# Two expert layers: router logits taken by tokens, one low part moved behind the choice, the first gather cut in two

## The reference

```python
def _hier_moe(x, w_grp, b_grp, w_exp, b_exp, w_gate, w_up, w_down):
    grp_logits = (xf @ w_grp + b_grp).astype(F32)           # 4 groups
    g_idx = jnp.argmax(grp_logits, axis=-1)
    exp_logits = (xf @ w_exp + b_exp).reshape(n, N_GROUPS, EXPERTS_PER_GROUP)   # 8 in each
    in_grp = take(exp_logits, g_idx)
    top_l, top_e = lax.top_k(in_grp, TOP_K_IN_GROUP)        # 2 experts of the token's group
    gate = p_grp * softmax(top_l)
    ...
    hdn = silu(xb @ w_gate[e]) * (xb @ w_up[e])             # 1024 -> 512, tokens of expert e
    y   = hdn @ w_down[e]                                   # 512 -> 1024, added back with its weight
```

## Time and profile before

| what | value |
|---|---|
| median of the runs | 2326.71 us (2326.80, 2326.71, 2320.91) |
| span of the profiled execution | 2323.1 us (the page gives no other time of that execution) |
| PE busy, PE weight loads | 2166.1 us (93%), 1528.0 us (66%) |
| DVE, ACT, POOL busy | 1142.2 us (49%), 784.0 us (34%), 61.5 us (3%) |
| loaded from memory | 619.5 MB, 267 GB/s over the span |
| mean granted clock of PE | 0.975 |
| experts of layer 0 and 1 | about 184 to 640 us, and 831 to 1291 us |

### The profile page before, as it was taken

One profiled execution on the slowest core, in us unless ns is written; L12 is line 12 of the kernel. 1 busy time (PEld: TensorE's weight loads), 2 busy tenths in 40 slices (PEclk: granted clock), 3 DMA queues, 4 the chain that ended last, 5 costly groups with the idle time before them and its releaser, 6 DMA issues.

```text
span 2323.1 us, 30109 instructions
## 1 busy us (share of the span) xinstructions
PE 2166.1 (93%) x12126; PEld 1528.0 (66%) x12126; DVE 1142.2 (49%) x1786; ACT 784.0 (34%) x1299; POOL 61.5 (3%) x62
## 2 busy tenths in 40 slices
PE   8999998899887989997988999999999999989998
PEld 7884443443367944433433688898888788888887
DVE  5582222121156831211111666678666766787666
ACT  3441110111034321101111355454555455554553
POOL 0010000000010100000000000001000000001000
PEclk9999999899998799999999999999999999999999
DMA  9449999999972289999999864634555464534561
GB/s 289 145 175 379 421 421 421 417 421 420 413 246 73 76 363 420 420 421 415 420 420 421 295 209 168 199 128 127 181 200 200 154 208 166 193 96 159 167 208 46
DMA packets 231542, 622.66 MB, mean 268 GB/s; under 512 B 15456, under 2 KB 166944, under 8 KB 182112
## 3 DMA queue, kind: packets, MB, share of 16 engines
q1 hardware_dynamic: 226096, 605.32, 68.7%
q0 software_dynamic: 3040, 10.78, 1.5%
q10 hardware_dynamic: 2256, 4.50, 0.5%
HBM read 619.51 MB, written 1.05 MB: 267 GB/s over the span
## 4 chain that ended last, share of the span: by engine, by line
PE 41%; DMA 6%; DVE 4%; ACT 2%; issue 1%; POOL 0%; SPq 0%; DVEq 0%; ACTq 0%
PE bank L1517 14%; PE bank L1505 10%; PE bank L1518 7%; PE bank L228 6%; PE bank L1345 3%; DMA arena<-in_moe_w_up 1%; DMA ring<-in_moe_w_up 1%; DMA ring<-in_ffn_gate 1%; DMA w_parts<-in_moe_w_up 1%; DMA x_tok<-in_moe_w_up 1%; DVE w_low L439 1%; PE bank L1673 1%; ACT w_high L432 1%; DVE x_tok L687 0%; DVE x_tok L676 0%
## 5 line engine op out<-in xcount | busy, mean ns | idle before, releaser
L439 DVE TENSOR_TENSOR w_low<-ring,w_high 128x1024 fp32r<-128x1024 f32 x364 | 441.1, 1225 | 271.7 <-ACT w_high L432 271.7
L1517 PE MATMUL bank<-xT_parts,w_high 128*128 128x512 f32 x1408 | 496.2, 395 | 6.0 <-DVE xT_parts L504 6.0
L432 ACT ACTIVATE w_high<-ring 128x1024 fp32r<-128x1024 f32 x364 | 377.1, 1053 | 218.0 <-PE bank L1518 184.6
L1518 PE MATMUL bank<-xT_parts,w_low 128*128 128x256 f32 x1408 | 394.5, 280 | 0.0
L1345 PE MATMUL bank<-ring,arena 128*64 128x512 f32 x1344 | 339.0, 594 | 17.3 <-DMA w_parts<-in_moe_w_gate 5.3
L1517 PEld LDWEIGHTS bank<-xT_parts,w_high 128*128 128x128 f32 x1408 | 264.0, 188 | 69.0 <-DVE xT_parts L504 6.9
L1345 PE MATMUL bank<-w_parts,arena 128*64 128x512 f32 x768 | 263.8, 609 | 13.4 <-DMA w_parts<-in_moe_w_up 6.7
L1518 PEld LDWEIGHTS bank<-xT_parts,w_low 128*128 128x128 f32 x1408 | 265.8, 189 | 3.1
L1345 PEld LDWEIGHTS bank<-ring,arena 128*64 128x64 f32 x1344 | 110.1, 137 | 230.5 <-issue 221.9
L1453 DVE SCALAR_TENSOR_TENSOR arena<-arena,bank 128x512 f32<-128x512 f32 x32 | 23.9, 747 | 434.1 <-PE bank L1345 434.1
L228 PE MATMUL bank<-w_high,xT_parts 128*128 128x256 f32 x1152 | 222.9, 290 | 10.4 <-DVE w_low L439 8.8
(11 more groups left out here) (284 smaller groups left out, 2934.4 us busy)
## 6 DMA issues: line engine op xcount, KB each, us to landing
ring<-in_moe_w_gate SPq DMA_DIRECT2D x56, 1024.0 KB, 24.3
ring<-in_moe_w_up SPq DMA_DIRECT2D x56, 1024.0 KB, 21.0
ring<-in_moe_w_down SPq DMA_DIRECT2D x56, 1024.0 KB, 25.8
ring<-in_ffn_gate SPq DMA_DIRECT2D x44, 1024.0 KB, 6.8
ring<-in_ffn_up SPq DMA_DIRECT2D x44, 1024.0 KB, 5.4
ring<-in_ffn_down SPq DMA_DIRECT2D x44, 1024.0 KB, 6.6
w_parts<-in_moe_w_up SPq DMA_DIRECT2D x32, 1024.0 KB, 26.1
w_parts<-in_moe_w_down SPq DMA_DIRECT2D x32, 1024.0 KB, 26.1
```

The lines of the kernel that those rows point to most:

```text
L432: e.activation(hi, src, ACT.Copy).then_inc(*S.high.tell(key))
L439: e.tensor_tensor(lo, src, hi.bitcast(F32), ALU.subtract).then_inc(*S.low.tell(key))
L1517: e.matmul(pairs(bank[:, :]), hi[:, j, :], k.x_parts[:, :, j, :], start=j == 0, stop=False)
L1518: ins = e.matmul(bank[:, 0:T], lo[:, j, :], k.xh[:, j, :], start=False, stop=j == KT - 1)
```

## The change

Three things are changed at the begin of both expert stages. First, the logits are taken with the tokens' high and low parts as the stationary side, 36 columns of router weights moving, so that they come out by tokens, and neither DVE's copy nor PE's turn is needed; the products of block 0 are put around the turning of block 1, and the `busy_pe` of 4 ahead of block 1 is gone there. Second, the low part of `x_tok`'s block 1 is done behind `chosen`, ahead of the wait for `places`. Third, the first gather of each `experts_pe` is cut: quarters 0 and 1, gate half 0, quarters 2 and 3, gate half 1, up, and only then `selT` and `weights`; ahead of the first wait of the main pass stands a `busy_pe` of 1. ACT's copies are split to match, with `selT` and `weights` behind silu.

```diff
 def route_pe(e, k, layer, n):
...
-    x_ready(e, k, n, 1)
-    mm(e, bank[:, 0:T], three([((hi[:, j, :], lo[:, j, :]), (k.xh[:, j, :], k.xl[:, j, :])) for j in range(KT)])
-       ).then_inc(*S.used.tell(("router", layer)))
-    view = route_turned(k, k.banks.open(e, A_BANKS, ("turned_logits", layer)))
-    e.wait_ge(*S.dve_out["logits", layer])
-    for b in range(NB):
-        ins = e.transpose(view[:, b, :], k.rot_tmp[0:N_LOGITS, block(b)], k.ident[0:N_LOGITS, 0:N_LOGITS])
-    ins.then_inc(*S.product.tell(("turned_logits", layer)))
+    transpose_block_pe(e, k, n, 0)
+    logits_high_pe(e, k, layer, n, 0)
+    transpose_block_pe(e, k, n, 1)
+    logits_low_pe(e, k, layer, n, 0)
+    logits_high_pe(e, k, layer, n, 1)
+    logits_low_pe(e, k, layer, n, 1)
     bank = k.banks.open(e, A_BANKS, ("places", layer))
     busy_pe(e, k, bank, 5)
...
+def logits_high_pe(e, k, layer, n, tb):
...
+    e.wait_ge(*S.low["router", layer])
+    e.wait_ge(*S.x_high[n, tb, 1])
+    mm(e, out, [(k.xh[:, j, block(tb)], w[:, j, 0:N_LOGITS]) for j in range(KT) for w in (hi, lo)], last=False)
+def logits_low_pe(e, k, layer, n, tb):
...
+    x_ready(e, k, n, tb)
+    ins = mm(e, logits_by_token(k.banks["logits", layer])[:, tb, :], [(k.xl[:, j, block(tb)], hi[:, j, 0:N_LOGITS]) for j in range(KT)], first=False)
+    if tb == NB - 1:
+        ins.then_inc(*S.used.tell(("router", layer)))
...
 def route_dve(e, k, layer):
...
-    token_parts_dve(e, k, layer)
+    token_low_dve(e, k, layer, 0)
+    view = logits_by_token(k.banks["logits", layer])
     e.wait_ge(*S.used["router", layer])
-    e.tensor_copy(k.rot_tmp[0:n, 0:T], k.banks["logits", layer][0:n, 0:T]).then_inc(*S.dve_out.tell(("logits", layer)))
-    view = route_turned(k, k.banks["turned_logits", layer])
-    e.wait_ge(*S.product["turned_logits", layer])
...
     e.tensor_tensor(R.hot, R.oh1, R.oh2, ALU.add).then_inc(*step.tell(("chosen", layer)))
+    token_low_dve(e, k, layer, 1)
     e.wait_ge(*S.product["places", layer])
...
-def gather_pe(e, k, X, G):
+def gather_x_pe(e, k, X, G, first, last):
-    for q in range(KT // 2):
+    for q in range(first, last):
         if q == 0:
+            if G == 0 and X.main:
+                busy_pe(e, k, bank, 1)
             e.wait_ge(*S.selected[X.key("slots", G)])
...
+def gather_rest_pe(e, k, X, G):
     view = pairs(X.banks.open(e, B_BANKS, X.key("selT", G))[:, :], GATHERED)
...
 def experts_pe(e, k, X, first, last):
-    gather_pe(e, k, X, first // GATHERED)
+    gather_x_pe(e, k, X, first // GATHERED, 0, KT // 4)
     for g in range(first, last):
...
-        if g % GATHERED == 0:
-            e.wait_ge(*S.act_out[X.key("xg", g // GATHERED, 2)])
-            e.wait_ge(*S.dve_out[X.key("xg", g // GATHERED, 3)])
-        paired_pe(e, k, X, [gate], "gate", g, KT // 2, xg)
+        for half in range(2):
+            if g == first and half == 1:
+                gather_x_pe(e, k, X, g // GATHERED, KT // 4, KT // 2)
+            if g % GATHERED == 0:
+                e.wait_ge(*S.act_out[X.key("xg", g // GATHERED, 2 * half)])
+                e.wait_ge(*S.dve_out[X.key("xg", g // GATHERED, 2 * half + 1)])
+            paired_pe(e, k, X, [gate], "gate", g, KT // 2, xg, (half,))
         up = X.banks.open(e, (1,), X.key("h", g))
         paired_pe(e, k, X, [up], "up", g, KT // 2, xg)
+        if g == first:
+            gather_rest_pe(e, k, X, g // GATHERED)
...
 def experts_act(e, k, X, first, last, ahead=None):
-    gather_act(e, k, X, first // GATHERED)
+    gather_x_act(e, k, X, first // GATHERED)
...
         e.activation(b.silu, X.banks[X.key("silu", g)][:, :], ACT.Silu).then_inc(*S.act_out.tell(X.key("silu", g)))
+        if g == first:
+            gather_rest_act(e, k, X, g // GATHERED)
...
-        transpose_x_pe(e, k, 0, "mixer")
...
-        transpose_x_pe(e, k, 2, "mixer")
```

More of the change, by code:

```diff
@@ L464, with transpose_block_pe @@
 BUSY = {"mixer": (0, 4), "experts": (4, 4), "ffn": (0, 4)}
+def transpose_block_pe(e, k, n, tb, busy=0):
+    S = k.S
+    if n < 0:
+        e.wait_ge(*S.x_loaded[tb][0])
+    for half in range(2):
+        view = pairs(k.banks.open(e, B_BANKS, ("xT", n, tb, half))[:, :], 4)
+        if half == 0:
+            busy_pe(e, k, k.banks["xT", n, tb, half], busy)
+        if n >= 0:
+            e.wait_ge(*S.x_tok[n, tb, half])
+        for i in range(4):
+            ins = e.transpose(view[:, i, :], k.x_tok[:, tb, block(4 * half + i)], k.ident)
+        ins.then_inc(*S.turned.tell((n, tb, half)))
 def transpose_x_pe(e, k, n, after=None):
-    S = k.S
     for tb in range(NB):
[L470 to L480, removed]
+        transpose_block_pe(e, k, n, tb, BUSY[after][tb] if n >= 0 else 0)
 def x_parts_at(k, n, tb, half):
@@ L1171, in route_dve @@
     e.wait_ge(*step["barred", layer])
-    e.wait_ge(*S.dve_out["turned_logits", layer])
+    e.wait_ge(*S.dve_out["logits", layer])
     e.tensor_tensor(el8, el8, bcast(R.goh.rearrange("p a g -> p (a g)"), PER_GROUP), ALU.add).then_inc(*step.tell(("in_group", layer)))
@@ L1256, in by_kk, with token_low_dve @@
     return v.rearrange("p (a k) -> p k a", k=KT)
-def token_parts_dve(e, k, layer):
+def token_low_dve(e, k, layer, tb):
     S = k.S
[L1261 to L1264, removed]
+    e.wait_ge(*S.token_high[layer, tb])
+    e.tensor_tensor(k.x_tok_low[:, tb, :, :], by_kk(k.x_tok[:, tb, :]), k.x_tok_high[:, tb, :, :].bitcast(F32), ALU.subtract
+                    ).then_inc(*S.token_low.tell((layer, tb)))
 def select_dve(e, k, X, G):
@@ L1332, in gather_dve, with paired_pe @@
         e.tensor_copy(b.xg[:, 2 * q:2 * q + 2, :], pairs(X.banks[X.key("xg", G, q)][:, :])).then_inc(*S.dve_out.tell(X.key("xg", G, q)))
-def paired_pe(e, k, X, tiles, name, g, per, lhs):
-    for half in range(2):
+def paired_pe(e, k, X, tiles, name, g, per, lhs, halves=(0, 1)):
+    for half in halves:
         chunks = [X.key(name, g, half, j) for j in range(PAIR)]
@@ L1391, in experts_pe @@
         gate = X.banks.open(e, (0,), X.key("silu", g))
-        if g % GATHERED == 0:
-            e.wait_ge(*S.act_out[X.key("xg", g // GATHERED, 2)])
-            e.wait_ge(*S.dve_out[X.key("xg", g // GATHERED, 3)])
-        paired_pe(e, k, X, [gate], "gate", g, KT // 2, xg)
+        for half in range(2):
+            if g == first and half == 1:
[4 more added lines that the diff above has]
+            paired_pe(e, k, X, [gate], "gate", g, KT // 2, xg, (half,))
         up = X.banks.open(e, (1,), X.key("h", g))
         paired_pe(e, k, X, [up], "up", g, KT // 2, xg)
+        if g == first:
+            gather_rest_pe(e, k, X, g // GATHERED)
         if gathered_after(g, last) is not None:
-            gather_pe(e, k, X, gathered_after(g, last))
+            gather_x_pe(e, k, X, gathered_after(g, last), 0, KT // 2)
+            gather_rest_pe(e, k, X, gathered_after(g, last))
         if g > first:
@@ L1424, in experts_act @@
         e.activation(b.silu, X.banks[X.key("silu", g)][:, :], ACT.Silu).then_inc(*S.act_out.tell(X.key("silu", g)))
+        if g == first:
+            gather_rest_act(e, k, X, g // GATHERED)
         if gathered_after(g, last) is not None:
[L1426 removed]
+            gather_x_act(e, k, X, gathered_after(g, last))
+            gather_rest_act(e, k, X, gathered_after(g, last))
         e.wait_ge(*S.product[X.key("hT", g)])
```

23 lines of the change are left out of this document (15 added, 8 removed).

## The result

The changed kernel takes 2328.78 us (median of 20 runs, 2323.45 to 2333.34) against 2324.81 for the kernel before (20 runs, 2320.72 to 2326.80): ratio 1.0019, 95% interval 1.0012 to 1.0026. It is slower by some 4 us (2.8 to 6.0). I had forecast 2326.0, which is no difference; the time lies inside the range that I gave, but off to the slower side. The profiled execution has a span of 2330.7 us and a time of its own of 2332.75; only two of its runs were longer, so the profile comes from the upper end of the kernel's scatter. Its numbers explain 7.6 us of span, more than the median's 4.

The account below looks back on a forecast made before the run. It took the DMA load stream as the bound, running dry for 5.5 and 7.0 us at the stages' begins. 0.8 lost in layer 0 and 0.7 won in layer 1 left 0.1 lost: forecast 2326.0 us, range 2319 to 2331.

Parts of the forecast that it names:

- The ruler: Load stream at a stage's begin: each release frees two slots, eight loads last 20.0 us; the start's shift is the whole effect.
- The stream's point: Until when the stream's new start is good: 30.6 and 32.1 us behind the first gather product before, 31.05 forecast.
- The clock's fall: In the logits, without wide products for some 10 us, PE's clock falls to 0.50 at about 168.
- for the narrow product I take 0.133, the 150 of 64 columns: Logits at the lower clock: 0.133 us a product from a 64-column row, so 32 products take 4.3.
- the other bound of mine: Upper price of a narrow logits product: 0.25 us, from 128 weights and 128 columns at the lower clock.
- my second rival: Narrow logits products cost 0.25 at the lower clock, 32 take 8.0; 7.5 us lost, 2334.2; chance 0.10.
- The clock's return: Full clock back 4.2 us after the five busy products ahead of places begin; PE free at 181.7, 1.35 too late.
- The fifth release: Slots freed by down half 0: 29.35 us behind the first gather product, effective 31.05, a third gap of 1.3.
- my sum of +0.1: Both layers' begins together: 0.8 us lost in layer 0, 0.7 won in layer 1, so 0.1 lost.
- the first release: Slots freed by gate half 0 after the cut gather: 6.65 us behind the first gather product, effective at 8.35.
- the three holes in the stream: Load stream at the stage's begin: three short dips instead of one long one; the later gaps 1.4 and 1.3 us.
- the first rival: Clock holds through the logits as PE is never idle for long: 3.5 us gained, 2323.2; chance 0.25.

Follow-up runs that it names:

- logits_three_quarters: Changed kernel with its new logits, but gather quarters 0 to 2, gate half 0, quarter 3, gate half 1, selT and weights, up, two busy products: 2326.05 us, ratio 1.0011.
- logits_wide: Changed kernel with all 128 columns of the router weights moving instead of 36: 2325.02 us against 2324.51 for the kernel before, ratio 0.9996.
- three_quarters_again: Kernel before, but gather quarters 0 to 2, gate half 0, quarter 3, gate half 1, selT and weights, up, two busy products; timed anew: 2320.84 us, ratio 0.9986.

## Why the prediction was wrong

**The ruler held for the loss.** The stream's point moved by +8.4 and the stages by +7.8. Over the kernels whose point became later it was right within 1.4 us. For those whose point became earlier it promised 0.6 to 3.0 us more than the stages gave; what takes that back I did not find.

**The clock's fall was right, its price was not.** It fell at about 170.2, 4.6 behind T, where I had 168, 3.4 behind T. That it would fall I had right; why it falls no run isolates. The failing step is "for the narrow product I take 0.133, the 150 of 64 columns". That row has 64 rows of weights and these have 128; the cost was 0.21, and 32 of them ran 6.8 us where I had 4.3. The turning ended 0.5 earlier than I had it, so that the logits were 1.9 late against my 10.9 behind T. The nearer row was the other bound of mine, 0.25 for 128 columns at the lower clock, since it has the same weights. The direction was that of my second rival, its 0.25 too high. That the profile's 7.6 is near this rival's 7.5 is luck: the rival had nothing of the late clock in the wait for the choice, nor of the slow first down, which make up half of it. The Trainium skill ("TensorE: Matmul & The Clock Gate", section "LDWEIGHTS (loading the stationary operand)") gives a weight load's time as the weights' columns divided by 1.2, in ns, whatever the rows: an estimate of 128/1.2 = 107 ns here. The spacing agrees at the full clock, 0.11, and is twice that at the lower one. For the rows the two measurements differ from it: 0.133 with 64 rows and 0.21 with 128, both at the lower clock and both with 128 columns of weights. The measurements decide; that it is the rows which make this difference no run isolates.

**The clock's return was late too.** I took it from down, 4.2 behind its begin; the windows show it back at about 184.0, 5.8 behind 178.19, and in layer 1 at 835.9, 5.0 behind the busy products' start at 830.87. In layer 0 they took 7.40 instead of 6.4, and PE was free 2.2 behind `chosen` where I had 1.35. This term is no fixed one: in `logits_three_quarters` the clock was back after 3.5 and 3.4, and the gather 1.4 and 1.2 us earlier. Together the gather is at 22.4 behind T against my 19.8: 2.55 late in layer 0 and 2.4 in layer 1.

**The fifth release** is 31.07 behind the gather and not 29.35. Up ended 0.35 late, L1492 began 1.86 behind it and not 1.66, and from there to the release were 9.0 and not 7.85, since down half 0 took 6.33 for 16 records and not the 5.35 from before: the clock stayed down through nearly all of it. By 2.55 + 1.7, and 2.4 + 1.6, the ruler is 8.3 worse than my sum of +0.1. That is the whole miss in this profile: of the 8.3 us some 4.0 are the late logits of the two layers, 1.0 the clock's return in the busy products, and 3.3 the fifth release.

**Right:** the first release 6.8 behind the gather (6.65 forecast), the three holes in the stream (not the fourth, short one ahead of them), the selection and weights on the path behind up, the load into `x_tok` at 185.21 hidden, the low part covered by the wait for the places. The rule that only long idle gaps cost the clock, which I weighed as the first rival (the Trainium skill, "TensorE: Matmul & The Clock Gate", section "Why this matters for your kernels"), fails here: the longest gap of PE between T and the fall was 0.83 us, until 167.44.

**What stays open:** the profile's loss is 7.6 and the median's 4.0. The changed kernel's runs spread over 9.9 us and those of before over 6.1; I have one profile of each. The profiled execution of the changed kernel is 4.0 above its median, which is nearly all of the difference. Its long runs are those with a low clock: the seven at a mean of 0.966 or 0.967, this one among them, took 2328.4 to 2333.3, the three at 0.973 and 0.974 took 2323.5 to 2328.1. A gather at 21.0 behind T in both layers, as in `logits_three_quarters`, would make it some 2.6 us shorter (an estimate from the two profiles). So the price of the narrow products is shown for every profile that has them, and what the late clock adds to it differs from run to run.

## What to carry to other kernels

Price a narrow product by its weights and by the clock it will really run at, and not by the columns that move; taking out a copy and a turn is no gain if it puts a longer run of slow products in front. A profile is of one execution: before you drop a theory for what it shows, look where this execution lies among the kernel's runs, as with `logits_wide`. Before reordering a begin, list which release of slots will be the latest in the new order: moving one forward is worth only the distance to the next. Here the selection and weights behind up hold back the latest release; behind gate half 0 the fifth release came 2.4 us earlier.

## What the hardware showed that I had not expected

Back-to-back products with 128 x 128 weights and 36 columns moving, with PE never idle from 171.37 to 178.19, ran at the lower clock throughout, and so did those with 128 columns in the profile of `logits_wide`; the clock came back only during the five busy products of 512 columns, 5.8 and 5.0 us behind their begin in the changed kernel, 3.5 and 3.4 in `logits_three_quarters`. And the clock can differ between two passes of the same instructions. In `three_quarters_again` the old logits, with 256 columns moving, ran at the full clock in layer 1 and mostly not in layer 0, and the gather was 0.8 us later:

```profile
168.00:172.00 4.00, 4.00 (x22) 4.00 (x23) 3.71 (x2) 3.98 (x4) 0.00 (x0) 0.57 1.00 418
...
815.50:819.50 4.00, 2.92 (x24) 2.72 (x23) 4.00 (x3) 3.98 (x4) 0.00 (x0) 1.00 1.01 417
```

A difference of a microsecond or two between two single profiles can be that, and no edit. It also shows that narrow products are not the only ones in whose course the clock falls.
